# Long convolutions of a hybrid encoder block: from 64-by-64 blocks staged in DRAM to 128-by-32 points reshuffled inside SBUF

## The chip, the cores and the metric

The kernel is written in Bass for one core of a Trainium2 chip. A core has a matrix engine (TensorE, PE), VectorE (DVE), ScalarE (ACT), GpSimd (POOL), a queue engine for transfers (SP) and 16 DMA engines. The metric is the device time of one execution in microseconds, the median of several.

## The reference

One encoder block over 2048 tokens of 1024 channels. RMSNorm, a projection, then two halves of 512 channels: a two-directional gated recurrence (LRU), and an order-2 Hyena recurrence with two long convolutions. Both are normed and projected out; then a mixture of 32 experts (top 2 within one of four groups) and a last RMSNorm.

```python
k = concat([hf, zeros(1), hb[1:][::-1]])        # 4096 taps, 2 orders, 512 channels
k = k / (sum(abs(k), axis=0) + EPS);  kf = rfft(k)
def _long_conv(z, kf, skip):
    y = irfft(rfft(z, n=2 * seq) * kf, n=2 * seq)[:, :seq]
    return y + z * skip
z = x1 * _long_conv(v, kf[:, 0], skip[0])
z = x2 * _long_conv(z, kf[:, 1], skip[1])
```

`hf` and `hb` come from a small network with sines over 33 features per position, times a decay. `v`, `x1` and `x2` are three-tap depthwise convolutions of the projection.

## The kernel before

The program is a row of phases. Each has a program for every engine, held together by counting semaphores, and begins by clearing its semaphores, so no phase overlaps the next. SP issues DMAs in the order written, and a wait on SP holds back all that stands behind it.

- `load_and_norm` (L83): norms x, turns it into `hT` and runs the sine network, whose result `zz` goes to DRAM (`ZZ`, L131). The 33 rows of `feats` are its first load (L118).
- `project_and_lru` (L226): four channel tiles, in each five projections of 8 x 4 products of 128x128 by 128x512 (`fill`, L361), gates, two scans, and the three-tap convolutions (`hyena_conv`, L491). The results v, x1, x2 are transposed and go to DRAM as `L`: three arrays of [128, 16, 512]; tile l holds tokens 16 p + l in row p.
- `filters` (L529): reloads `zz`; for each of 32 tiles GpSimd spreads it over a masked `zb` (L582), TensorE makes the taps of both orders (`generate`, L609), VectorE multiplies with the decay (L660) and takes the magnitude (L663), GpSimd sums it (L589), TensorE transforms (`transform`, L615), ScalarE copies (L639) and stores `KA`. At the end VectorE forms the reciprocal norm `invn`.
- For each of the two orders three phases. `conv_forward` (L671): 32 products over the points n1, results to DRAM as `SA`. `conv_blocks` (L717): 32 blocks, in each a load of five tables (`mats`, L743), z and k (`zin`, `kin`, L745) of 128 rows of 2 KB, then five full products (L758, L763, L764), two multiplications by the spectrum on VectorE (L803), a copy and a store of `qo` to DRAM (`SI`). `conv_inverse` (L806): `stage` is loaded back, two products per tile (L840), scale by `invn`, add the skip, apply the gate, and in order 1 transposes and a store of `YT`.
- `output_projection` (L977): 16 tiles. SP loads `yt` and the rows of x (`xt`, L1036, L1051), TensorE makes 48 split products per tile, VectorE adds x (L1186) after it has waited once for five small loads of router weights, biases and gain (`w_in_`, L1029, L1214).
- `route`, `experts`: not touched.
- `combine` (L1600): 16 tiles, for each a load of x2 (`xcomb`, L1621), two indirect gathers of expert rows (L1645), sums, norm, and a store of 512 KB to the output (L1627) with two buffers.

## Time and profile before

| | us |
|---|---|
| median of 3 runs | 2717.03 (2716.83 to 2722.48) |
| profiled execution | 2722.55, span 2720.8 |

| engine | busy us | share of the span |
|---|---|---|
| PE | 2319.1 | 85% |
| DVE | 1418.7 | 52% |
| ACT | 1067.5 | 39% |
| POOL | 316.8 | 12% |

The profile counts 531.74 MB of transfers, 195 GB/s over the span. An f32 product of 128x512 is recorded as two matrix instructions. "DMA share" is the mean busy share of the 16 DMA engines; packets are booked by their start, so a short stretch can show over 1. Time stamps are microseconds from the span's start.

### The profile page before, as it was taken

To read this page: it belongs to the slowest core of one execution; us is meant where nothing else is said; L and a number is where in the kernel's file an instruction comes from. 1 tells how busy PE (TensorE), PEld (TensorE's weight loads), DVE (VectorE), ACT (ScalarE), POOL (GpSimd) and SP (SyncE) were. 2 spreads that over 40 slices of the span, in tenths; PEclk is the share of its full clock that TensorE was granted. 3 is DMA by queue.
4 is the path that set the end of the run, shared out by engine and by line. 5 is a ranking of instruction groups with operands and counts; after the bars stand their busy time and mean duration, and the time that the engine had idled before them with its cause. 6 is when DMAs were issued, how large, how long until landed. Compare 5 with 4: busy or idle time off the path is not lost. (4 is left out here: it accounts for less than half of the span.)

```text
span 2720.8 us, 33071 instructions
## 1 busy us (share of the span) xinstructions
PE 2319.1 (85%) x8253; PEld 1455.2 (53%) x8254; DVE 1418.7 (52%) x1238; ACT 1067.5 (39%) x1342; POOL 316.8 (12%) x337
## 2 busy tenths in 40 slices
PE   2699999999879599679849994699999999999940
PEld 1344444444333244234327873588878788788830
DVE  4357291745679123312244445446486864655447
ACT  4232221414122322032222221456586965766533
POOL 0000000000078300420120000000000000000023
PEclk8899999999989799789869997799999999999975
DMA  3122313121266488378743431667598986786648
GB/s 152 34 79 64 100 47 108 33 73 58 62 214 217 173 276 280 143 276 290 276 173 111 153 136 57 246 230 290 220 388 310 395 310 240 277 309 217 261 185 355
DMA packets 263770, 531.74 MB, mean 195 GB/s; under 512 B 27311, under 2 KB 98195, under 8 KB 259347
## 3 DMA queue, kind: packets, MB, share of 16 engines
q1 hardware_dynamic: 221812, 390.76, 41.1%
q10 hardware_dynamic: 30112, 97.53, 9.0%
q0 software_dynamic: 11808, 43.00, 4.2%
q8 instruction: 17, 0.28, 0.0%
q14 instruction: 21, 0.17, 0.0%
HBM read 390.69 MB, written 140.51 MB: 195 GB/s over the span
## 5 line engine op out<-in xcount | busy, mean ns | idle before, releaser
L361 PE MATMUL pj<-hT,W 128*128 128x512 f32 x1280 | 553.7, 594 | 2.7 <-DMA W<-in_w_in_dram 2.7
L361 PEld LDWEIGHTS pj<-hT,W 128*128 128x128 f32 x1280 | 243.0, 191 | 304.3 <-issue 304.3
L1458 PE MATMUL p<-wh_hi,x_hi 128*128 128x512 f32 x768 | 309.0, 402 | 11.2 <-DVE wh_lo L1583 11.1
L1583 DVE TENSOR_TENSOR wh_lo<-w_raw,wh_hi 128x2048 fp32r<-128x2048 f32 x128 | 284.8, 2287 | 51.5 <-ACT wh_hi L1547 48.8
L1458 PE MATMUL p<-wh_lo,x_hi 128*128 128x512 f32 x768 | 304.2, 396 | 0.0
L1458 PE MATMUL p<-wh_hi,x_lo 128*128 128x512 f32 x768 | 304.1, 396 | 0.0
L1547 ACT ACTIVATE wh_hi<-w_raw 128x2048 fp32r<-128x2048 f32 x128 | 234.7, 1914 | 0.3 <-DMA w_raw<-in_exp_w_dram 0.2
L803 DVE TENSOR_TENSOR u<-pr,zs 128x512 f32<-128x512 f32 x64 | 44.3, 692 | 287.4 <-ACT zs L778 167.5
L1458 PEld LDWEIGHTS p<-wh_hi,x_hi 128*128 128x128 f32 x768 | 144.6, 188 | 49.5 <-DVE wh_lo L1583 15.0
L1458 PEld LDWEIGHTS p<-wh_hi,x_lo 128*128 128x128 f32 x768 | 144.7, 188 | 35.0
L1458 PEld LDWEIGHTS p<-wh_lo,x_hi 128*128 128x128 f32 x768 | 144.8, 189 | 32.7
L1458 PE MATMUL pyy<-wy_hi,a_hi 128*128 x392 | 160.0, 408 | 2.3 <-ACT yb L1529 2.3
L1458 PE MATMUL pyy<-wy_lo,a_hi 128*128 x392 | 155.5, 397 | 0.0
L1458 PE MATMUL pyy<-wy_hi,a_lo 128*128 x392 | 155.3, 396 | 0.0
L1583 DVE TENSOR_TENSOR wy_lo<-w_raw,wy_hi 128x2048 fp32r<-128x2048 f32 x64 | 143.6, 2285 | 0.0
L1594 DVE TENSOR_TENSOR a<-p,s 128x512 f32<-128x512 f32 x48 | 33.2, 692 | 204.2 <-ACT s L1556 204.2
L406 ACT ACTIVATE hraw<-pj 128x512 f32<-128x512 f32 x48 | 28.7, 597 | 265.1 <-PE pj L361 265.1
L1547 ACT ACTIVATE wy_hi<-w_raw 128x2048 fp32r<-128x2048 f32 x64 | 119.3, 1911 | 2.4 <-DMA w_raw<-in_exp_w_dram 1.5
L1428 POOL COPY curidx<-idx 128x1 int32 (+1 forms) x50 | 9.1, 183 | 870.3 <-PE px L1466 795.3
L1556 ACT ACTIVATE s<-p 128x512 f32<-128x512 f32 x48 | 28.9, 601 | 207.6 <-PE p L1458 207.3
L758 PE MATMUL pz<-zin,mats 128*128 128x512 f32 x128 | 67.9, 613 | 32.8 <-DMA kin<-scratch_KA 32.8
L783 ACT ACTIVATE qo<-pq 128x512 f32<-128x512 f32 x64 | 38.2, 597 | 139.0 <-PE pq L764 139.0
(266 smaller groups left out, 3796.2 us busy)
## 6 DMA issues: line engine op xcount, KB each, us to landing
w_raw<-in_exp_w_dram SPq DMA_DIRECT2D x512, 256.0 KB, 4.6
w_raw<-in_exp_w_dram SPq DMA_DIRECT2D x128, 512.0 KB, 9.6
scratch_YB<-yb ACTq DMA_DIRECT2D x50, 512.0 KB
mats<-in_mats_dram SPq DMA_DIRECT2D x64, 320.0 KB, 3.2
scratch_YB<-zero SPq DMA_DIRECT2D x4, 4096.0 KB, 14.6
scratch_KA<-kst ACTq DMA_DIRECT2D x32, 512.0 KB, 3.5
scratch_SA<-stage ACTq DMA_DIRECT2D x8, 2048.0 KB, 6.7
zin<-scratch_SA SPq DMA_DIRECT2D x64, 256.0 KB, 4.1
```

The source lines that it names most:

```text
L361: last = pe.matmul(pj[n][:, :], lhs(k), rhs(k, n), start=(k == 0), stop=(k == n_k - 1))
L406: ins = act.activation(out(n), pj[n][:, :], func)
L758: pe.matmul(bank_[s % 2][:, :], mats[:, s, m, :], rhs[:, s, :], start=True, stop=True).then_inc(fwd, 1)
L783: act.activation(qo[:, s, :], pq[s % 2][:, :], ACT.Copy).then_inc(q_evac, 1)
L803: dve.tensor_tensor(dst[:, s % 2, :], src[s % 2][:, :], zs[:, s % 2, :], ALU.mult).then_inc(uv_ready, 1)
L1428: pool.tensor_copy(cur[:, :], idx[:, ds(B + LEAD, 1)]).then_inc(idx_ready, 1)
L1458: mm = pe.matmul(acc[:, :], x[:, k, :], w, start=(k == 0 and i == 0), stop=(k == n - 1 and i == 2))
L1547: act.activation(place, raw[:, j:j + 2, :], ACT.Copy).then_inc(rounded, 1)
L1556: act.activation(s1[:, :], p1[:, :], ACT.Silu).then_inc(s_ready, 1)
L1583: dve.tensor_tensor(lo, raw[:, j:j + 2, :], hi.bitcast(F32), ALU.subtract).then_inc(lowered, 1)
L1594: dve.tensor_tensor(a[:, :], p3[:, :], s1[:, :], ALU.mult).then_inc(a_ready, 1)
```

## The change

1. Order of phases: `load_and_norm`, `filters`, `project_and_lru`, one phase `conv`, `output_projection` and on. `zz` stays in SBUF, laid out twice with zeros (`zzd`), so nothing is masked or reloaded. The magnitude moves to ScalarE, in one instruction for both orders. The skip is added to tap 0 in units of the norm, and 1/norm is folded into the taps of x1 and x2 in `project_and_lru`.
2. 4096 points are 128 by 32 instead of 64 by 64. Tiles are l of 16, tokens 32 n + 2 l + g in row (g, n); the three-tap convolutions write in that order (`by_parity`), and x and the output are read and stored through the same order, as `[2, 64, 1024]`.
3. `conv`: both orders in one phase. Forward products have 64 rows of contraction, spectrum products 64 output columns, so that each uses half of the array, in pairs. 16 pairs per order; the tables (2 MB forward, 2 MB inverse) are loaded once.
4. `stage` ([128, 32, 512]) stays in SBUF. A pair's signal is copied from four partitions of it to 128 partitions of `zin`, twice per pair, the result back to four partitions, twice per pair. `KA` is read as four rows of 64 KB in the same way.

```diff
-            act.activation(zz[0:R, :], arg[0:R, :], ACT.Sin).then_inc(mlp_sin, 1)
+            act.activation(zzd[0:R, 0, :], arg[0:R, :], ACT.Sin).then_inc(mlp_sin, 1)
...
-                    conv(step, hc[:, slot, :], hraw[:, slot, :], 3, Q_HW + which, 3, Q_HB + which, hc_ready)
+                    conv(step, hc[:, slot, :].rearrange("p (g m) -> p g m", g=2), hraw[:, slot, :],
+                         3, Q_HW + which, 3, Q_HB + which, hc_ready, by_parity)
...
+                dve.tensor_tensor(tile(j), pk[j % 2][:, :, :], dec[:, j % 4, :].unsqueeze(1).broadcast_to([P, 2, CH]), ALU.mult).then_inc(k_ready, 1)
...
+        def rows(a, p, t):
+            first = (p & 1) * 64 + (p >> 1 & 1) * 32 + t * 16 + (p >> 2)
+            return a[first:first + 13:4]
...
+            def load_k(n):
+                for t in range(2):
+                    sp.dma_start(kin[:, n % 3, t, :], rows(dram["KA"][n // PAIRS], n % PAIRS, t)).then_inc(kin_in[n % 3], 16)
+
+            def load_z(n):
+                for t in range(2):
+                    sp.dma_start(zin[:, n % 3, t, :], rows(stage, n % PAIRS, t)).then_inc(zin_in[n % 3], 16)
+
+            def store_q(n):
+                sp.wait_ge(q_evac, n + 1)
+                for t in range(2):
+                    sp.dma_start(rows(stage, n % PAIRS, t), qo[:, n % 2, t, :]).then_inc(q_out[n % 2], 16)
+
+            def blocks(o):
+                sp.wait_ge(a_act, NT * (o + 1))
+                sp.wait_ge(a_dve, NT * (o + 1))
+                for n in range(o * PAIRS, o * PAIRS + 3):
+                    load_z(n)
+                for n in range(o * PAIRS, o * PAIRS + PAIRS):
+                    sp.wait_ge(z_mm, 2 * n + 2)
+                    if n + 3 < (o + 1) * PAIRS:
+                        load_z(n + 3)
+                    if n + 3 < 2 * PAIRS:
+                        sp.wait_ge(k_mm, n + 1)
+                        load_k(n + 3)
+                    if n > o * PAIRS:
+                        store_q(n - 1)
+                store_q((o + 1) * PAIRS - 1)
...
+            def spread(bank, t, src, free):
...
+                for g in range(2):
+                    h = slice(g * HALF, g * HALF + HALF)
+                    pe.matmul(bank[:, g, :], fs[h, :], src[h], start=True, stop=True).then_inc(a_mm, 1)
...
+            def k_product(n):
...
+                for r in range(2):
+                    for t in range(2):
+                        h = slice(t * HALF, t * HALF + HALF)
+                        last = pe.matmul(pk[n % 2][h, r, :], fwd[:, 2 * p + t, r * HALF:r * HALF + HALF], kin[:, n % 3, t, :], start=True, stop=True)
...
+            def inverse(n):
...
+                for r, y, done in ((0, yr, yr_ready), (1, yi, yi_ready)):
+                    pe.wait_ge(done, n + 1)
+                    for t in range(2):
+                        h = slice(t * HALF, t * HALF + HALF)
+                        last = pe.matmul(pq[:, t, :], inv[h, p, r, :], y[h, n % 2, :], start=(r == 0), stop=(r == 1))
...
+                for r, out in ((0, by_r), (1, by_i)):
...
+                    dve.tensor_tensor(out[:, n % 2], pk[n % 2][:, :, :], zs[:, n % 2, r, :].unsqueeze(1).broadcast_to([P, 2, CH]), ALU.mult).then_inc(prod, 1)
...
-        x_t = dram["x"].rearrange("o (p l) d -> l p (o d)", l=NT)
+        x_t = dram["x"].rearrange("o (n l g) d -> l g n (o d)", g=2, l=NT)
...
-        out_t = dram["out"].rearrange("o (p l) d -> l p (o d)", l=NT)
+        out_t = dram["out"].rearrange("o (n l g) d -> l g n (o d)", g=2, l=NT)
...
-                sp.dma_start(out_t[ds(t, 1)].rearrange("a p d -> (a p) d"), out[:, q % 2, :]).then_inc(o_out[q % 2], 16)
+                sp.dma_start(out_t[ds(t, 1)].rearrange("a g n d -> (a g) n d"), out[:, q % 2, :]).then_inc(o_out[q % 2], 16)
```

In order, the one phase loads tables, four groups of `L` and the first three k (`ring` holds three groups of four tiles), spreads v into `stage` (16 tiles), runs the 16 pairs of order 0, then alternates `collect` (inverse over n1, times the gate) with the next `spread`, runs the 16 pairs of order 1, and collects again with transposes and the store of `YT`. GpSimd makes the real part of the product from the two products of VectorE, which makes the imaginary part.

## Rows read from the trace of the kernel before

**Rows 1.** Busy time by stage: stretch, length, then each engine's us (instructions), clock, DMA.
```profile
core 0: us, PE busy (x) PEld busy (x) DVE busy (x) ACT busy (x) POOL busy (x), PEclk, DMA share, GB/s
...
90.00:760.00 670.00, 631.69 (x1623) 292.42 (x1621) 357.12 (x156) 168.69 (x232) 3.50 (x8) 0.97 0.24 71
...
749.70:905.00 155.30, 123.69 (x260) 48.35 (x260) 132.13 (x134) 38.23 (x64) 109.34 (x98) 0.92 0.57 200
...
905.00:947.00 42.00, 30.23 (x64) 13.00 (x64) 0.00 (x0) 18.46 (x32) 20.31 (x16) 0.83 0.51 208
947.00:1099.00 152.00, 140.64 (x320) 61.79 (x320) 42.12 (x64) 38.22 (x64) 0.00 (x0) 0.95 0.79 262
1099.00:1142.00 43.00, 30.50 (x64) 13.16 (x64) 21.88 (x32) 0.00 (x0) 24.26 (x16) 0.82 0.49 198
...
1422.00:1672.00 250.00, 230.05 (x1182) 191.52 (x1182) 104.78 (x184) 65.87 (x127) 17.87 (x30) 0.98 0.36 123
...
2625.00:2720.80 95.80, 0.00 (x0) 0.00 (x0) 63.79 (x80) 31.89 (x56) 39.32 (x32) 0.50 0.91 356
```

**Rows 2.** Waits in the block part, 947 to 1099: who waited, us, times, longest.
```profile
ACT qo L783 <- PE pq L764: 69.5, 32, 2.8
...
PE pz L758 <- DMA kin<-scratch_KA: 16.5, 1, 16.5
```

**Rows 3.** Timeline: starts of phases, of VectorE's splits, and combine's first store.
```profile
749.70 0.34 SPq L560 DMA_DIRECT2D zz<-scratch_ZZ  x1
...
903.69 0.34 SPq L683 DMA_DIRECT2D faz<-in_fa_signal_dram  x1
...
1397.54 2.12 SPq L1032 DMA_DIRECT2D wo<-in_w_out_dram  x4
...
1414.17 0.74 DVE L1210 TENSOR_SCALAR wo_hi<-wo,gAB 128x1024 fp32r<-128x1024 f32 x1
...
2625.21 0.34 SPq L1619 DMA_DIRECT2D gain_fin<-in_norm_final_g_dram  x1
...
2645.31 0.36 SPq L1627 DMA_DIRECT2D out_dram<-outt  x1
```

**Rows 4.** Groups of instructions: projection and filters; busy us, mean ns, idle before.
```profile
L361 PE MATMUL pj<-hT,W 128*128 128x512 f32 x1280 | 553.7, 594 | 2.7 <-DMA W<-in_w_in_dram 2.7
...
L663 DVE SCALAR_TENSOR_TENSOR ka<-kt 128x512 f32<-128x512 f32 x64 | 85.1, 1329 | 4.3
L589 POOL TENSOR_TENSOR acc<-acc,ka 128x512 f32<-128x512 f32 x64 | 81.1, 1267 | 24.3 <-DVE ka L663 24.3
...
L660 DVE TENSOR_TENSOR kt<-pk,dec 128x512 f32<-128x512 f32 x64 | 43.4, 679 | 11.2 <-PE pk L609 11.2
...
L639 ACT ACTIVATE kst<-pa 128x512 f32<-128x512 f32 x64 | 38.2, 597 | 114.2 <-PE pa L615 114.2
```

**Rows 5.** Groups of instructions: the same VectorE shape, strided and contiguous.
```profile
L524 DVE TENSOR_TENSOR Tb<-Tf,If 128x2048 f32<-128x2048 f32 x4 | 15.1, 3773 | 58.0 <-ACT If L406 58.0
...
L520 DVE TENSOR_TENSOR Tf<-Tf,Tb 128x2048 f32<-128x2048 f32 x4 | 9.2, 2293 | 0.1
```

**Rows 6.** DMA issues: transfer, issuer, count, KB each, median us to landing.
```profile
mats<-in_mats_dram SPq DMA_DIRECT2D x64, 320.0 KB, 3.2
...
zin<-scratch_SA SPq DMA_DIRECT2D x64, 256.0 KB, 4.1
kin<-scratch_KA SPq DMA_DIRECT2D x64, 256.0 KB, 4.6
scratch_SI<-qo ACTq DMA_DIRECT2D x64, 256.0 KB, 4.2
...
xt<-in_x_dram SPq DMA_DIRECT2D x16, 512.0 KB, 5.1
...
out_dram<-outt SPq DMA_DIRECT2D x16, 512.0 KB, 5.5
```

**Rows 7.** Stretches: `feats` in flight, loads of X, experts, combine; columns as in rows 1.
```profile
5.00:5.60 0.60, 0.00 (x0) 0.00 (x0) 0.00 (x0) 0.00 (x0) 0.00 (x0) 1.00 0.77 288
14.00:18.00 4.00, 4.00 (x6) 1.65 (x5) 0.00 (x0) 0.00 (x0) 0.00 (x0) 1.00 1.02 418
...
1972.00:2040.00 68.00, 67.36 (x312) 54.30 (x310) 57.35 (x38) 57.74 (x51) 4.60 (x8) 1.00 1.03 388
...
2640.00:2700.00 60.00, 0.00 (x0) 0.00 (x0) 46.79 (x60) 23.71 (x42) 31.76 (x24) 0.50 1.02 395
```

More of the change, by code:

```diff
@@ L22 @@
 R = 64
-HALF = R // 2
+N1, N2 = P, N // P
+HALF = N1 // 2
+PAIRS = N2 // 2
 NT = 16
@@ new lines, in _, with magnitude, evacuate @@
+        @block.scalar
+        def _(act):
+            def magnitude(j):
+                act.wait_ge(k_ready, j + 1)
+                if j >= 2:
+                    act.wait_ge(summed, j)
+                act.activation(ka[:, j % 2], tile(j), ACT.Abs).then_inc(abs_ready, 1)
+            def evacuate(i):
+                act.wait_ge(fa_done, i + 1)
+                if i >= 4:
+                    act.wait_ge(kst_out[i % 4], 16 * (i // 4))
+                act.activation(kst[:, i % 4], pa[i % 2][:, :, :], ACT.Copy).then_inc(kst_ready, 1)
+            magnitude(0)
+            magnitude(1)
+            for j in range(2, N2):
+                magnitude(j)
+                evacuate(j - 2)
+            evacuate(N2 - 2)
+            evacuate(N2 - 1)
@@ new lines, in z_product @@
+            def z_product(n):
+                p = n % PAIRS
+                pe.wait_ge(zin_in[n % 3], 32 * (n // 3) + 32)
+                if n:
+                    pe.wait_ge(zs_ready, 2 * n)
+                for r in range(2):
+                    for t in range(2):
+                        h = slice(t * HALF, t * HALF + HALF)
+                        last = pe.matmul(pz[h, r, :], fwd[:, 2 * p + t, r * HALF:r * HALF + HALF], zin[:, n % 3, t, :], start=True, stop=True)
+                    last.then_inc(z_mm, 1)
@@ new lines, in blocks, with collect @@
+            def blocks(o):
+                first = o * PAIRS
+                k_product(first)
+                for n in range(first, first + PAIRS):
+                    z_product(n)
+                    if n + 1 < first + PAIRS:
+                        k_product(n + 1)
+                    if n > first:
+                        inverse(n - 1)
+                inverse(first + PAIRS - 1)
+            def collect(out, l, free):
+                if free > 0:
+                    pe.wait_ge(gated, free)
+                for g in range(2):
+                    h = slice(g * HALF, g * HALF + HALF)
+                    last = pe.matmul(out[h, :], ia[:, :], stage[:, 2 * l + g, :], start=True, stop=True)
+                last.then_inc(i_mm, 1)
@@ new lines, in _ @@
+            pe.wait_ge(tables_in, 32)
+            for l in range(NT):
+                if l % 4 == 0:
+                    pe.wait_ge(ring_in[l // 4 % 3], 16 * (l // 12) + 16)
+                spread((*pk, pz, pq)[l % 4], l, ring[:, l // 4 % 3, l % 4, :], l - 3)
+            pe.wait_ge(fwd_in, 16)
+            pe.wait_ge(a_act, NT)
+            pe.wait_ge(a_dve, NT)
+            pe.wait_ge(inv_in, 16)
+            blocks(0)
+            for s in range(2):
+                pe.wait_ge(q_out[s], 32 * (PAIRS // 2))
@@ new lines, in _ @@
+            LAG = 2
+            for l in range(NT + LAG):
+                if l < NT:
+                    collect(pq[:, l % 2, :], l, l - 1)
+                if l >= LAG:
+                    t = l - LAG
+                    pe.wait_ge(gated, t + 1)
+                    spread((pz, *pk)[t % 3], t, z[:, t % 4, :], NT + t - 2 if t >= 3 else 0)
+            pe.wait_ge(a_act, 2 * NT - 2)
+            pe.wait_ge(a_dve, 2 * NT - 2)
+            blocks(1)
+            for s in range(2):
+                pe.wait_ge(q_out[s], 32 * PAIRS)
@@ new lines, in result, with blocks @@
+            def result(n):
+                act.wait_ge(inv_mm, n + 1)
+                if n >= 2:
+                    act.wait_ge(q_out[n % 2], 32 * (n // 2))
+                act.activation(qo[:, n % 2], pq[:, :, :], ACT.Copy).then_inc(q_evac, 1)
+            def blocks(o):
+                first = o * PAIRS
+                for n in range(first, first + PAIRS):
+                    signal(n)
+                    if n > first:
+                        result(n - 1)
+                result(first + PAIRS - 1)
@@ new lines, in gate @@
+            def gate(out, t, G0, free):
+                G = G0 + t // 4
+                dve.wait_ge(i_mm, (G0 // GROUPS - 1) * NT + t + 1)
+                dve.wait_ge(ring_in[G % 3], 16 * (G // 3) + 16)
+                if t >= 4:
+                    dve.wait_ge(free, 2 * (NT + t - 3) if free is a_mm else t - 3)
+                dve.tensor_tensor(z[:, t % 4, :], out, ring[:, G % 3, t % 4, :], ALU.mult).then_inc(gated, 1)
+            for l in range(NT):
+                evacuate((*pk, pz, pq)[l % 4], l, l)
```

677 lines of the change are left out of this document (298 added, 379 removed).

## The prediction

> **What bounds the kernel now.** I read the busy time by stage first [rows 1]. The change touches five of these stages. The filters (749.7 to 905) keep VectorE busy 132 of 155 us and TensorE 124. A long convolution has a forward part (42 us), a block part (152 us) and an inverse part (43 us); the second repeats it. In the block part TensorE is busy 141 of 152 us at a DMA share of 0.79, so it is TensorE's stage with DMA close behind. The waits say the same: ScalarE waits for the product, and the only long wait for a transfer is the first, 16.5 us [rows 2]. The forward and inverse parts have TensorE busy 30 us of 42 to 43; the rest is the start of a phase. The output projection (1422 to 1672) is TensorE's, with DMA at 0.36. The last stage, combine, has DMA at 0.91 over its whole length and no TensorE work: there the transfers set the time. Projection with the LRU (90 to 760) is TensorE's, 632 of 670 us.
>
> **Filters, moved ahead of the projection.** The zero-padded `zz` makes the masked copies on GpSimd unnecessary. A tile still needs two generating and two transforming products. A full f32 product of 128x512 is two records; 1280 of them take 553.7 us, so one product costs 0.865 us [rows 4] and a tile 3.46 us. Before, VectorE set the pace with two of 0.68 and two of 1.33 us = 4.0 us [rows 4]. The magnitude now goes to ScalarE and VectorE keeps about 1.36 us a tile; GpSimd has 2 x 1.27 = 2.5, ScalarE about 2 x 0.6 + 1.1 = 2.3 (the kst row, and its like for the magnitude). TensorE becomes the bound: 32 x 3.46 = 111 us. Around it: some 8 us for loads and first tiles, and a tail that is new, because tile 0 is transformed only after the norm: last product, magnitude, sum, ones products, eight small ones, the skip added, transform, store: about 18 us; then 4 us to the next phase. 141 us, against 154 from 749.7 to 903.7 [rows 3]: **-13 us** (-25 to +10). The store of ZZ and its reload go; they lay in the head of the old stage.
>
> **Projection.** The same products. VectorE reads its three-tap convolutions at a stride of two. Its one strided operation here takes 3.79 us against 2.29 for a contiguous one of the same shape [rows 5], so a convolution may cost up to 4 us more, three times per channel tile. VectorE is busy 357 of 670 us [rows 1], and the last operation of each tile waits 58.0/4 = 14.5 us for a gate that TensorE makes last [rows 5]. That idle time hides 12 us: 0 (0 to +10 if the cover fails in one tile). The folding of the norm into the taps is two tiny operations in the setup: 0.
>
> **Long convolutions: what TensorE saves.** Before, 32 blocks of five products, 4.3 us each, twice: 280 us of TensorE [rows 1]. Now 16 pairs with four spectrum, four signal and four inverse products that each use half of the array. If the two halves run together a pair costs 6 x 0.865 = 5.2 us, if not 10.4 us. Nothing in this trace shows two half-array products side by side. The mats (64 x 320 KB [rows 6]) go too. The Trainium skill, TensorEngine Tiling (Array Packing), Key Properties, says that tiles run loads and products in parallel, and that changing the tiling mode drains the engine; no run here shows either.
>
> **Long convolutions: what the transfers cost.** Here is the point on which I decide. Each pair moves z in, k in and q out as 2 x 256 KB each, and each of these DMAs has one side of only **four rows** (four partitions of `stage`, or four rows of `KA`) of 64 KB, where the old ones had 128 rows [rows 6]. The trace has one large transfer with few rows, the 33 rows of `feats`: in its fullest stretch it moved 288 GB/s, where four 2 MB loads of 128 rows move 418 [rows 7]. 288/418 is 11.0 of 16, and 11 is the largest divisor of 33 up to 16. So I read: the outermost dimension is dealt out evenly, and a DMA of four rows gets four engines, always with the others idle. The other reading (33 rows are just a short burst) would leave all 16. The Trainium skill, DMA: Bandwidth & Descriptors, Why a DMA increments its semaphore by 16 and not by 1, states it: the engine count is the largest up to 16 that divides the slowest dimension of both sides, and the lowest-numbered engines are used. The 288 GB/s agree; by its rule the change loses what the shared engines lose, and this speaks against the change.
>
> The price: 192 DMAs of 256 KB are 50.3 MB. Saturated 2 KB and 4 KB traffic moves 388 GB/s [rows 7], 24.2 per engine, so four engines move 97 GB/s and need 520 us. The same engines also carry their sixteenth of 12 MB of L, 4 MB of tables and 4 MB of YT, 21 MB at 395 to 418 GB/s: 51 us. Where these engines stand still: 7 us at the start, 5 at the end of the first spread (its last ring slot is queued behind six k loads), 10 and 12 at the two block tails where z, products, inverse and store follow one another, 28 in the middle collect and spread (16 tiles of about 2 us less its ring loads), 25 in the last collect with transposes and 3 for landings: 90 us. Together 661 us. Before, from 903.7 to 1397.5 [rows 3], 494 us. **+167 us**. Ends: 20.7 GB/s per engine (block part: 262/16/0.79 [rows 1]) gives 608 in place of 520, +255; 26.1 (418/16) gives 482, +129. TensorE's 5.2 or 10.4 us per pair lie under 16 us of transfer, and so do VectorE (2 x 1.36 + 0.68), ScalarE (2.3) and GpSimd (1.3). If the halves do not run together only the spreads and collects grow, by about 60 us.
>
> What waits behind: SP issues everything in order. A z load waits for `z_mm`, a k load for `k_mm`, and the store of q behind both; three z and three k are ahead, 32 us of queue, so a stall of TensorE is not felt.
>
> **Output projection.** x is now read as [2, 64, 1024], two outer rows: by the same reading two engines, 256 KB each, at 24.2 to 26.1 GB/s 10 to 10.6 us; with a sixteenth of 1.5 MB of other traffic on the same engines 14 us a tile, against 250/16 = 15.6 us. A load is issued after the tile two before it is done and has about 18 us until VectorE adds it, so in the steady state it just hides. At the start two such loads stand ahead of the router weights and the gain on SP's queue, for all of which VectorE waits: wo 10 + x 20 + yt 5 us from 1400 makes 1436 to 1438, where the eight splits of wo, 2 us each from 1414, end near 1430 [rows 3]: **+8 us** (0 to +50).
>
> **Combine.** The output is stored as [2, 64, 1024] too. Before, 32 MB at 395 GB/s [rows 7] was the bound. On the two engines a tile now is 256 KB of store, 32 KB of x and 64 KB of gathered rows: 352 KB at 25 GB/s, 14 us. From the first store, 20 us into the stage [rows 3], 16 stores of 10.4 us, 12 loads of 1.3 and some 22 gathers of 1.3: 166 + 16 + 26 = 208 us. 228 us against 95.8: **+132 us** (+110 to +150; 0 if the store uses all engines).
>
> **Sum.** -13 + 0 + 167 + 8 + 132 = +294 us. The profiled execution took 2722.6 us (span 2720.8), the median is 2717.0; on the median this gives **3011 us**. Nothing in experts or routing changes: the tiles hold other tokens, but the slots of the experts are as many.
>
> **Rivals.**
> All sixteen engines take every DMA (the 33 rows mislead). A pair is then 1.57 MB at 262 GB/s [rows 1], 6.0 us, above TensorE's 5.2: 192 us, with 95 us for spreads, collects and transposes and 35 us of starts and tails 322: -172, filters -13, nothing else: 2532 us. For it: the full stretch of those 33 rows lasts 0.6 us, one sample. Against it: 288 GB/s where 33 rows would keep sixteen engines busy as well.
> The same, but half-array products don't overlap, so that the change doesn't do what it says: 10.4 us per pair, 333 us, and 150 + 35 around it: 518, +24 - 13: 2728 us.
> Four engines in the convolutions but all of them for x and the output (the two-row side is merged or split on the way): 2717 - 13 + 167 = 2871 us.
> The slow side beyond my sum: SBUF to SBUF copies that read one partition per engine and write another run at half the rate of the rows, 12 GB/s. 128 of the 192 DMAs (z and q) then take twice 347 us: 3011 + 347 = 3358 us. It decides as soon as one engine's rate from a single partition falls below 20 GB/s. No row shows SBUF to SBUF.
>
> **How the numbers follow.** Forecast as summed 0.66; forecast with halves that don't overlap (about 3071) 0.08; few engines only in the convolutions 0.07; half rate 0.05; sixteen engines 0.11; sixteen without overlap 0.03. The terms' ends, not all at once on one side, give 2940 to 3150 for the first two. To leave out no more than 0.2 the range takes in 2871: 2860 to 3160; outside lie the sixteen engines (0.14 in all) and the half rate (0.05). About 0.2% is what a measurement of this kernel can tell from no change: faster 0.11, within 0.01 (of the last case), slower 0.88.
>
> **What the profile would show.** The block stretches at a DMA share near 0.25 and about 97 GB/s with TensorE busy a third, and TensorE waiting for `zin`; z landing after 15 us or more instead of 4; combine near 228 us at about 150 GB/s with ScalarE waiting for the store of outt; filters near 141 us with TensorE busy all of it. The forecast is wrong if the blocks show a DMA share over 0.7, or if an x load lands in 5 us as before [rows 6].

## The result and the profile after

The changed kernel takes 2987.2 us (median), the kernel before 2719.7 us beside it: ratio 1.098, 95% interval 1.096 to 1.100. It is slower by 267 us. The profiled execution took 2989.0 us, its span is 2987.3. One of the four runs, 3459.8 us long with a granted clock of 0.70 on the mean against 0.88 in the others, is left out of the ratio; the other three lie between 2983.7 and 2989.0.

Timeline of the changed kernel, SP's queue, the first transfer of each phase (start us, us, engine and line, transfer). They answer to [rows 3]: the phases now start with the filters at 97.8 and the projection at 233.5.

```profile
97.81 1.12 SPq L564 DMA_DIRECT2D w<-in_hy_filt_w_dram  x2
...
233.50 0.34 SPq L281 DMA_DIRECT2D prow<-in_lru_conv_w_dram  x1
...
882.88 0.36 SPq L745 DMA_DIRECT2D fs<-in_fa_signal_dram  x1
...
1519.34 2.07 SPq L1095 DMA_DIRECT2D wo<-in_w_out_dram  x4
...
1801.32 0.34 SPq L1323 DMA_DIRECT2D tri<-in_tri_dram  x1
...
2761.81 0.34 SPq L1682 DMA_DIRECT2D gain_fin<-in_norm_final_g_dram  x1
```

From one start to the next, beside the kernel before and the prediction:

| stage | before | after | change | predicted |
|---|---|---|---|---|
| load and norm | 100.9 | 97.8 | -3.1 | 0 |
| filters | 154.0 | 135.7 | -18.3 | -13 |
| projection, LRU | 648.8 | 649.4 | +0.6 | 0 |
| long convolutions | 493.9 | 636.5 | **+142.6** | +167 |
| output projection | 269.8 | 282.0 | +12.2 | +8 |
| routing, experts | 957.9 | 960.5 | +2.6 | 0 |
| combine | 95.6 | 225.5 | **+129.9** | +132 |
| sum | | | +266.5 | +294 |

The changed kernel by stretch, columns as in [rows 1]: the filters, the blocks of the first convolution, the middle (collect and spread), the blocks of the second, the steady output projection, combine from its first store on, and the end of combine, where its last store is alone.

```profile
97.80:233.50 135.70, 117.64 (x276) 65.31 (x276) 42.35 (x37) 64.15 (x65) 77.52 (x37) 0.92 0.54 190
...
928.29:1195.76 267.47, 121.66 (x384) 33.95 (x384) 50.13 (x49) 35.17 (x48) 28.95 (x17) 0.72 0.28 106
1100.00:1180.00 80.00, 37.74 (x112) 10.77 (x112) 12.19 (x12) 10.12 (x14) 7.42 (x5) 0.71 0.26 98
1195.76:1232.02 36.26, 36.23 (x133) 9.41 (x135) 22.13 (x32) 9.55 (x16) 0.00 (x0) 0.92 0.31 103
1232.02:1477.03 245.01, 120.05 (x382) 33.44 (x379) 50.15 (x49) 35.20 (x48) 28.97 (x17) 0.73 0.26 99
...
1541.00:1791.00 250.00, 228.25 (x1146) 189.59 (x1147) 105.58 (x181) 62.42 (x122) 17.81 (x30) 0.96 0.35 126
2782.00:2938.00 156.00, 0.00 (x0) 0.00 (x0) 46.95 (x60) 22.77 (x40) 28.21 (x22) 0.50 0.45 154
...
2975.00:2987.00 12.00, 0.00 (x0) 0.00 (x0) 0.00 (x0) 0.00 (x0) 0.00 (x0) 0.50 0.12 49
```

Read the blocks against [rows 1]: there TensorE was busy 141 of 152 us with DMA at 0.79 and 262 GB/s. Now no engine is busy half of the time, and DMA, which looks idle at 0.26, is the bound: 0.26 of sixteen is four engines. Combine fell from 0.91 and 356 GB/s to 0.45 and 154. Its 0.45 is no count of engines, since the loads of x2 and the gathered rows are in it; the last store, alone, shows 0.12 and 49 GB/s, two engines of sixteen.

Waits of the changed kernel, first in the blocks of the first convolution (928 to 1195), then in the whole of combine (who waited, us, times, longest):

```profile
PEld ck L788 <- DMA kin<-scratch_KA: 114.7, 13, 10.0
```

```profile
ACT outt L1718 <- DMA out_dram<-outt: 150.5, 14, 16.8
```

In [rows 2] TensorE waited 16.5 us for a transfer, once. Now it waits 13 times for k, which stands behind z in SP's queue of z, k, q. That queue, one pair of blocks (timeline of SP):

```profile
1098.75 5.27 SPq L722 DMA_DIRECT2D zin<-stage  x2
1104.06 5.15 SPq L718 DMA_DIRECT2D kin<-scratch_KA  x2
1109.25 5.09 SPq L727 DMA_DIRECT2D stage<-qo  x2
```

Each group of two takes SP 5.1 to 5.3 us here, for 512 KB, and up to 5.9 elsewhere in the blocks. From 1250.33 to 1410.96 ten pairs were issued, 16.06 us a pair of 1.57 MB: 98 GB/s.

### The profile page after: what moved, and what is told of

It reads as the page before. It is cut to its first block and busy times, and to the rows that moved or that the text cites. A ratio compares the mean times of both kernels' runs of the same rounds, so it can differ in the third digit from the quotient of the medians.

```text
span 2987.3 us, 30293 instructions
## 1 busy us (share of the span) xinstructions
PE 2232.7 (75%) x8397; PEld 1389.6 (47%) x8398; DVE 1358.1 (45%) x1130; ACT 1059.8 (35%) x1262; POOL 252.3 (8%) x243
## 5 line engine op out<-in xcount | busy, mean ns | idle before, releaser
L1521 PE MATMUL p<-wh_hi,x_hi 128*128 128x512 f32 x768 | 308.9, 402 | 11.2 <-DVE wh_lo L1646 11.1
L788 PE MATMUL ck<-kin,fwd_b 128*64 128x512 f32 x256 | 106.0, 976 | 216.6 <-DMA kin<-scratch_KA 205.7
L942 DVE TENSOR_TENSOR by_r<-ck,zs 128x1024 f32<-128x1024 f32 x32 | 39.2, 1224 | 362.5 <-ACT zs L886 362.5
L892 ACT ACTIVATE qo<-cq 128x1024 f32<-128x1024 f32 x32 | 32.7, 1023 | 375.3 <-PE cq L811 326.5
L922 POOL TENSOR_TENSOR yr<-by_r,by_i 128x512 f32<-128x512 f32 x32 | 56.6, 1767 | 1170.0 <-DVE by_i L942 1170.0
L788 PEld LDWEIGHTS ck<-kin,fwd_b 128*64 128x64 f32 x256 | 23.3, 202 | 278.6 <-DMA kin<-scratch_KA 228.6
```

The source lines that it names most:

```text
L788: last = pe.matmul(pk[n % 2][h, r, :], fwd[:, 2 * p + t, r * HALF:r * HALF + HALF], kin[:, n % 3, t, :], start=True, stop=True)
L892: act.activation(qo[:, n % 2], pq[:, :, :], ACT.Copy).then_inc(q_evac, 1)
L922: dif = pool.tensor_tensor(yr[:, n % 2, :], by_r[:, n % 2, 0, :], by_i[:, n % 2, 1, :], ALU.subtract)
L942: dve.tensor_tensor(out[:, n % 2], pk[n % 2][:, :, :], zs[:, n % 2, r, :].unsqueeze(1).broadcast_to([P, 2, CH]), ALU.mult).then_inc(prod, 1)
L1521: mm = pe.matmul(acc[:, :], x[:, k, :], w, start=(k == 0 and i == 0), stop=(k == n - 1 and i == 2))
```

## The experiments

My theory was that of the prediction: the outermost dimension of a transfer's two sides sets how many DMA engines take part, as the largest number up to 16 that divides it on both sides. In every run below the smaller of the two counts divides the larger, so what happens when it does not stays open. The rivals: copies from SBUF to SBUF, or few partitions at one end, are slow in themselves; scattered rows or patterns of two levels are slow; SP's in-order issue or the half-array products hold the period. Where no ratio is given, the kernel was run once; repeated runs of one kernel lay within 0.4% of each other, 10 us, so small differences are read from the stages of the trace.

### Rows of the x loads and of the output

```diff
-                sp.dma_start(out_t[ds(t, 1)].rearrange("a g n d -> (a g) n d"), out[:, q % 2, :]).then_inc(o_out[q % 2], 16)
+                for g in range(2):
+                    sp.dma_start(out_t[ds(t, 1)][:, g].rearrange("a n d -> (a n) d"), out[64 * g:64 * g + 64, q % 2, :]).then_inc(o_out[q % 2], 16)
```

The x loads of the output projection are split alike, and the waits count two DMAs per tile.

> The changed kernel with one edit in two stages: each x load of the output projection and each output store of combine goes out as two DMAs of 64 rows instead of one of 2 x 64. The same bytes to the same addresses, twice as many DMAs. Theory (the outermost dimension of a pattern is dealt out over the engines, so two outer rows get two engines and 64 get all sixteen): combine falls from 225.5 us to the 96 us of the kernel before, the output projection from 282 to 270, nothing else moves, 2987 - 142 = 2845 us. Rival (the 4 KB rows of the output lie every 32nd row of DRAM, and that scatter or the store itself is slow): the rows lie as before, both stages stay, 2987 us. Rival (SP's issue of each DMA costs): slower by 28 x 0.6 us.

Measured: 2851.7 us against 2720.3 before, ratio 1.049 (1.047 to 1.050). Combine took 102.6 us, the output projection 273.8. Twice as many stores, and combine is less than half as long. The stretch of its combine between stores, and its longest wait:

```profile
2770.00:2830.00 60.00, 0.00 (x0) 0.00 (x0) 40.35 (x53) 21.45 (x38) 25.13 (x19) 0.50 0.99 365
```

```profile
ACT outt L1722 <- DMA out_dram<-outt: 40.5, 14, 5.3
```

The same bytes went to the same addresses, so scatter in DRAM is out. SP's issue costs nothing either. Combine kept 7 us over the kernel before: between its stores it moves 365 GB/s, where that kernel moved 395 [rows 7]. Why is open.

### Rows of k

```diff
-                    sp.dma_start(kin[:, n % 3, t, :], rows(dram["KA"][n // PAIRS], n % PAIRS, t)).then_inc(kin_in[n % 3], 16)
+                    first = (n % PAIRS) * 8 + t * 4
+                    sp.dma_start(kin[:, n % 3, t, :], dram["KA"][n // PAIRS][first:first + 4].rearrange("i n c -> (i n) c")).then_inc(kin_in[n % 3], 16)
...
+    FK = F
     F, IA = F[:, np.argsort(place)], IA[np.argsort(place)] / N
...
-    out = dict(fa_filter=F, ...)
+    out = dict(fa_filter=FK, ...)
```

> The changed kernel with KA in the natural order of the spectrum, so that four consecutive rows of 64 KB are 128 rows of 2 KB: the k loads have 128 outer rows instead of four; z and q keep four. Same bytes. Theory (four engines carry z, k and q; a pair of 1.57 MB took 15.4 us, 25.5 GB/s per engine): z and q leave 1.05 MB for the four engines, 10.3 us, and a sixteenth of k on each adds 1.3: 11.6 us a pair, 32 x 3.8 = -122 us, 2865 us. Rival (the copies from SBUF to SBUF are the slow ones, bound by the few partitions at one end, and k only waits in line behind them): the period falls by less than the 1.3 us that k would take on sixteen engines at full rate, under -45 us. Rival (SP's in-order issue, or the waits of the block chain, set the period): 0.

Measured: 2884.6 us, ratio 1.060 (1.058 to 1.062); the convolutions took 533.8 us, -102.7. The expectation was on a period of 15.4 us that I had read from too short a stretch; over ten pairs it is 16.1. Here it is 13.3. SP's queue, one pair:

```profile
1049.24 5.06 SPq L723 DMA_DIRECT2D zin<-stage  x2
1054.35 3.16 SPq L719 DMA_DIRECT2D kin<-scratch_KA  x2
1057.55 4.91 SPq L728 DMA_DIRECT2D stage<-qo  x2
```

and two stretches of such a pair, first with a k passing, then with z alone (columns as in [rows 1]):

```profile
1044.00:1048.00 4.00, 4.00 (x14) 1.09 (x12) 0.00 (x0) 0.00 (x0) 0.00 (x0) 0.74 0.60 174
1050.00:1054.00 4.00, 0.00 (x0) 0.00 (x0) 3.05 (x3) 0.48 (x1) 1.49 (x1) 0.87 0.26 98
```

k went to more engines, z and q stayed at four and at their pace. But k kept 3.2 us of the queue, not the 1.3 that its bytes need. From a block part's first z to the first ring load behind it the two parts are 46.1 and 37.6 us shorter, together 84 of the 103; the rest is the head, where six k loads stood ahead of the ring loads: the first z is issued 26.7 us after the phase starts, in the changed kernel 45.4. The rival "SBUF to SBUF" had foreseen under 45 us; it is weakened, not out.

### z issued by GpSimd

```diff
-                    sp.dma_start(zin[:, n % 3, t, :], rows(stage, n % PAIRS, t)).then_inc(zin_in[n % 3], 16)
+                    pool.dma_start(zin[:, n % 3, t, :], rows(stage, n % PAIRS, t)).then_inc(zin_in[n % 3], 16)
```

with the waits for `a_act`, `a_dve` and `z_mm` moved to GpSimd's stream.

> The changed kernel with the z loads issued by GpSimd (its software queue) instead of SP; patterns, bytes and waits are the same. Theory: all four-row DMAs of SP's queue use the same four engines. If GpSimd's queue deals its four-row DMAs to other engines, k and q keep 1.05 MB on the four, and z adds its share: 11.6 us a pair if z goes round all engines, 10.3 if it has four others, conv -120 to -160 us, 2830 to 2865 us. If GpSimd's queue uses the same four: no change in the block stretches, 15.4 us a pair. Rival (the partitions of stage are the limit, whoever issues): 15.4 us too; then the next run but one, z through DRAM, tells them apart.

Measured: 2918.6 us, the convolutions 569.0, -67.5. A stretch of its blocks:

```profile
1000.00:1100.00 100.00, 51.89 (x176) 14.65 (x172) 24.04 (x24) 16.45 (x24) 23.60 (x24) 0.76 0.39 118
```

Over 100 us the share is 0.39 and 118 GB/s pass, where with SP alone it stays at 0.26 and 98; in single stretches it is 0.54 (1058.5 to 1060), in others 0.26 (1050 to 1052). So the same four-row copies ran in part beside SP's on other engines, and the partitions of `stage` were not the limit. The Trainium skill, DMA: Bandwidth & Descriptors, Why a DMA increments its semaphore by 16 and not by 1, says that GpSimd's queue takes its engines in turn. The changing share agrees with that; which engines they were no view shows. The gain was about half of what I expected. GpSimd waited 87.5 us for TensorE's z product (12 times, 950 to 1150) before it could issue; whether that or the queue's own pace took the other half stays open.

### One prime number

The kernel before, with other shapes for its output store.

```diff
+        out_4 = dram["out"].rearrange("o (n g l) d -> l g n (o d)", l=NT, g=4)
...
-                sp.dma_start(out_t[ds(t, 1)].rearrange("a p d -> (a p) d"), out[:, q % 2, :]).then_inc(o_out[q % 2], 16)
+                if t < 12:
+                    n = (P, 127, 126)[t // 4]
+                    sp.dma_start(out_t[t][0:n], out[0:n, q % 2, :]).then_inc(o_out[q % 2], 16)
+                else:
+                    sp.dma_start(out_4[t], out[:, q % 2, :]).then_inc(o_out[q % 2], 16)
```

> The kernel before (not the changed one) with four shapes of output store in combine: tiles 0 to 3 with 128 rows as they were, 4 to 7 with 127 rows (the last row of each tile is left out), 8 to 11 with 126 rows (the last two are left out), 12 to 15 with the same 128 rows as four outer rows of 32 (rows interleaved by four, so that part of the output is in another order). The count of engines is the largest one up to 16 that divides the outermost dimension, is the theory: 127 is prime, one engine, 508 KB at 25.5 GB/s are 20 us and with that engine's share of the loads 24 us a tile; 126 gives 14 engines and is like 128, 6 us a tile; four rows give four, 5.1 us plus 3.9 of loads, 9 us, or 5.1 once no load is left. Stage 96 + 4 x 18 + about 6 = 174 us, the whole 2800 us. Rival (a pattern of two levels is slow, all engines take part): 127 and 126 are like 128, only the last four are longer, stage under 115 us, 2740 us. Rival (engines are filled in turn whatever the count): nothing changes, 2720 us.

Measured: 2813.3 us, +93; the stage 189.6 us, 16 more than expected. Timeline of its stores: the four of 127 rows, the first two of 126.

```profile
2663.22 0.28 SPq L1630 DMA_DIRECT2D out_dram<-outt  x1
2677.63 1.26 SPq L1630 DMA_DIRECT2D out_dram<-outt  x1
2699.87 0.37 SPq L1630 DMA_DIRECT2D out_dram<-outt  x1
2719.10 7.65 SPq L1630 DMA_DIRECT2D out_dram<-outt  x1
2748.66 1.39 SPq L1630 DMA_DIRECT2D out_dram<-outt  x1
2766.05 0.36 SPq L1630 DMA_DIRECT2D out_dram<-outt  x1
```

One row less, in a plain pattern of one level, and a tile takes 14 to 30 us, 21.4 on the mean ((2748.66 - 2663.22) / 4). With one more row less, once the slow ones have drained, the next two stores follow 4 us apart (2770.02, 2773.99). The rivals foresee no such step between 128 and 127 rows. The last four, of four outer rows, took 7.6 us each to the end of the span, between my two values.

### All of it through DRAM, with 128 rows and with four

Two kernels that share one edit: a spread tile of `stage` goes to a DRAM buffer SZ, z is loaded from there, q goes to SQ and comes back into `stage`. In the first SZ, KA and SQ are read and written as 128 rows, in the second with the changed kernel's four. The edit of the first:

```diff
-                    sp.dma_start(zin[:, n % 3, t, :], rows(stage, n % PAIRS, t)).then_inc(zin_in[n % 3], 16)
+                    first = (n % PAIRS) * 8 + t * 4
+                    sp.dma_start(zin[:, n % 3, t, :], dram["SZ"][first:first + 4].rearrange("i n c -> (i n) c")).then_inc(zin_in[n % 3], 16)
...
-                    sp.dma_start(rows(stage, n % PAIRS, t), qo[:, n % 2, t, :]).then_inc(q_out[n % 2], 16)
+                    first = (n % PAIRS) * 8 + t * 4
+                    sp.dma_start(dram["SQ"][first:first + 4].rearrange("i n c -> (i n) c"), qo[:, n % 2, t, :]).then_inc(q_out[n % 2], 16)
...
+                sp.dma_start(dram["SZ"][:, 2 * l:2 * l + 2, :], stage[:, 2 * l:2 * l + 2, :]).then_inc(sz_out, 16)
...
+                    sp.dma_start(stage[:, 4 * g:4 * g + 4, :], dram["SQ"][:, 4 * g:4 * g + 4, :]).then_inc(st_in[g], 16)
```

> The changed kernel without its SBUF to SBUF copies: each spread tile of stage is stored to DRAM (128 rows of 4 KB), z is loaded as 128 rows of 2 KB, q goes to DRAM as 128 rows and comes back into stage in eight loads; KA in the natural order as in e2_k128. Half-array products, one phase and everything else stay. 32 MB of transfers more. Theory (rows, hence engines): a pair is 1.57 MB on sixteen engines, 4 to 6 us, so TensorE's three groups of 1.94 us, 5.8 us, or the chain z, evacuation, products, GpSimd, inverse set the period at about 7 us instead of 15.4; spreads and collects as before, four turns of store and load cost 6 us each: conv 395 us instead of 636, 2987 - 241 = 2746 us. If the turns and the extra 32 MB weigh more, up to 2800. Rival (the half-array products or the block chain hold the period near 15 us): conv stays above 620 us, 2970 us or more.

> As e5_dram, z and q through DRAM, but every z, k and q transfer keeps the changed kernel's pattern of four outer rows of 64 KB on its DRAM side (KA in its permuted order). Nothing goes from SBUF to SBUF, and the bytes per pair are the same. Theory (four rows, four engines, wherever the rows lie): the period stays at 15.4 us a pair at 98 GB/s, and the four turns through DRAM come on top: conv 640 to 670 us, 2990 to 3020 us. Rival (a copy from SBUF to SBUF, or from and to only four partitions, is what is slow): z and q are faster here, the period falls below 12 us, the whole is under 2900 us.

Measured: with 128 rows 2717.5 us, 28 less than expected, ratio 0.9997 (0.9988 to 1.0007) to the kernel before, the convolutions 366.3 us. With four rows 3028.3 us, the convolutions 674.2. The blocks of each, 128 rows first:

```profile
965.00:1050.00 85.00, 73.91 (x304) 22.94 (x300) 39.37 (x41) 27.48 (x37) 21.24 (x12) 0.92 0.77 274
```

```profile
950.00:1180.00 230.00, 120.92 (x381) 33.71 (x382) 50.15 (x49) 34.23 (x47) 28.98 (x17) 0.73 0.26 100
```

With nothing from SBUF to SBUF the four rows give the same 0.26 and 100 GB/s, and 15.8 us a pair (z at 1061.17, 1077.01, 1092.86, 1108.63). With 128 rows a pair takes 5.5 us (z at 974.85, 980.37, 985.85), and TensorE is the bound again, busy 74 of 85 us. So the new convolutions, half-array pairs, one phase and tables loaded once together, are worth -128 us against [rows 3]'s 493.9, once the engines are there. How much of it each of the three gives was not divided.

### From SBUF to SBUF with all partitions

```diff
-                    sp.dma_start(zin[:, n % 3, t, :], rows(stage, n % PAIRS, t)).then_inc(zin_in[n % 3], 16)
+                    sp.dma_start(zin[:, n % 3, t, :], stage[:, 2 * (n % PAIRS) + t, :]).then_inc(zin_in[n % 3], 16)
```

and q back alike; k as 128 rows. The kernel leaves out the spreading of four partitions over 128, so its convolutions compute nothing meaningful.

> The changed kernel with k as in e2_k128, and with z and q still copied from SBUF to SBUF, the same bytes in as many DMAs, but partition to partition: zin takes tile 2p + t of stage with its 128 partitions in place, and q goes back there. It leaves out the transpose between partitions, so the convolution's values mean nothing; only its time counts. Theory (the four outer rows are the cause, not the memory at either end): all engines take part, the period falls from e2's 13.3 us to TensorE's 5.5 us as in e5_dram, and without the four turns through DRAM the convolutions take about 335 to 355 us, 2690 to 2705 us in all. Rival (SBUF to SBUF is slower than DRAM even with all rows): the period stays above 8 us, conv above 440 us.

Measured: 2663.1 us, the convolutions 312.8. SP's queue, one pair, 5.5 us to the next:

```profile
978.93 1.26 SPq L723 DMA_DIRECT2D zin<-stage  x2
980.24 1.09 SPq L719 DMA_DIRECT2D kin<-scratch_KA  x2
983.27 1.11 SPq L728 DMA_DIRECT2D stage<-qo  x2
```

That closes a square: SBUF or DRAM, four rows or 128. With four rows the memory moves the period by 0.3 us (16.1 and 15.8); the rows move it by 10. With 128 rows TensorE sets the 5.5 us, so a difference between the memories would not show. My lower bound of 335 was too high by 22 us; I did not divide that further.

### The law by itself

The kernel before with 18 single stores behind its last one. `to` is one tile of a scratch buffer in DRAM.

```diff
+            for n, g in ((128, 1), (127, 1), (126, 1), (121, 1), (128, 8), (125, 5), (128, 4), (126, 3), (128, 2)):
+                for _ in range(2):
+                    dst = to[0:n].rearrange("(n g) d -> g n d", g=g) if g > 1 else to[0:n]
+                    sp.dma_start(dst, out[0:n, 0, :]).then_inc(law_out, 16)
+                    done += 16
+                    sp.wait_ge(law_out, done)
```

> The kernel before, with 18 more DMAs appended after its last store: one buffer of outt goes to a scratch buffer in DRAM, one DMA at a time, each waited for before the next, two of each shape: 128 rows of 4 KB; 127; 126; 121; 128 as 8 outer rows of 16; 125 as 5 of 25; 128 as 4 of 32; 126 as 3 of 42; 128 as 2 of 64. Theory: engines = the largest number up to 16 that divides the outermost dimension of both sides, 25.5 GB/s each, and about 2 us to issue and land. From issue to the next issue: 16 engines 3.3 us; 127 rows one engine 22.4; 126 rows 14 engines 3.4; 121 rows 11 engines 3.8; eight 4.6; five 6.0; four 7.1; three 8.8; two 12.3. Together +143 us, 2863 us. Rival (two levels in a pattern are slow in themselves, the count of rows does not matter): 127, 126 and 121 rows all within 0.3 us of 128, and the five two-level shapes all alike.

Measured: 2875.2 us. A stretch inside each shape's stores, in the order 128, 127, 126, 121 rows, then 8, 5, 4, 3, 2 outer rows; the last two columns are the share of 16 engines and the GB/s (the short stretches hold a bit of a store's start or end):

```profile
2719.60:2721.00 1.40, 0.00 (x0) 0.00 (x0) 0.00 (x0) 0.00 (x0) 0.00 (x0) 0.50 0.91 375
2730.00:2740.00 10.00, 0.00 (x0) 0.00 (x0) 0.00 (x0) 0.00 (x0) 0.00 (x0) 0.50 0.06 26
2766.80:2768.00 1.20, 0.00 (x0) 0.00 (x0) 0.00 (x0) 0.00 (x0) 0.00 (x0) 0.50 0.91 311
2773.20:2775.20 2.00, 0.00 (x0) 0.00 (x0) 0.00 (x0) 0.00 (x0) 0.00 (x0) 0.50 0.68 168
2782.00:2786.00 4.00, 0.00 (x0) 0.00 (x0) 0.00 (x0) 0.00 (x0) 0.00 (x0) 0.50 0.46 113
2795.00:2799.00 4.00, 0.00 (x0) 0.00 (x0) 0.00 (x0) 0.00 (x0) 0.00 (x0) 0.50 0.31 98
2808.50:2816.50 8.00, 0.00 (x0) 0.00 (x0) 0.00 (x0) 0.00 (x0) 0.00 (x0) 0.50 0.22 61
2829.00:2836.00 7.00, 0.00 (x0) 0.00 (x0) 0.00 (x0) 0.00 (x0) 0.00 (x0) 0.50 0.19 64
2850.00:2860.00 10.00, 0.00 (x0) 0.00 (x0) 0.00 (x0) 0.00 (x0) 0.00 (x0) 0.50 0.12 47
```

The shares fit 16, 1, 14, 11, 8, 5, 4, 3 and 2 sixteenths, within the idle edges; 126 rows can't be told from 128 here. But the times from issue to issue are as expected only at the ends: 2.6 (3.3 expected), 22.3 (22.4), 3.1 (3.4), 4.3 (3.8), 6.1 (4.6), 6.9 (6.0), **10.2 (7.1)**, 9.9 (8.8), 12.9 (12.3). Four rows cost more than three. Two runs more were for this.

```diff
-                    dst = to[0:n].rearrange("(n g) d -> g n d", g=g) if g > 1 else to[0:n]
+                    dst = dram["X2"][0:g, 0:n // g] if g > 1 else dram["X2"][0][0:n]
```

> As e9_law, with one difference: the five shapes of two levels write blocks of rows to DRAM (8 blocks of 16 adjacent rows, 5 of 25, 4 of 32, 3 of 42, 2 of 64, each block in another tile of the scratch buffer), where in e9_law row i of block b lay next to row i of block b + 1, so that engines wrote neighbouring 4 KB rows at once. In e9_law the share of busy engines followed the count (0.22 to 0.25 for four) but four rows took 10.2 us instead of the 7.1 expected, and eight 6.1 instead of 4.6. Theory (the interleaved rows slow each engine, the count stands): here 8 rows take 4.6 us or less, five 5.5, four 6.5, three 8.3, two 11.8, from 1.3 us plus 25 GB/s per engine; the five pairs save about 17 us in all. Rival (a pattern of four or eight outer rows is slow per engine wherever the rows lie): the five times are those of e9_law: 6.1, 6.9, 10.2, 9.9, 12.9 us.

Measured: 2876.1 us, and from issue to issue 6.1, 7.0, 10.2, 9.9 and 12.9 us: the same. My guess that neighbouring rows in DRAM disturb each other was wrong, its rival right.

```diff
-                for _ in range(2):
+                for r in range(4):
...
-                    sp.wait_ge(law_out, done)
+                sp.wait_ge(law_out, done)
```

(each of the four to a place of its own)

> As e11_law_blocks, but four DMAs of each shape go out one behind the other, to different places, and only the fourth is waited for: 36 DMAs. e11_law_blocks gave the same times as e9_law, so the place of the rows in DRAM is not what made four rows take 10.2 us where 25.5 GB/s per engine give 5.1 + 1.3, while in the convolutions four-row DMAs queued behind each other moved 98 GB/s. Theory (the loss is at the start of a DMA that finds its engines idle): a group of four takes 1.3 us, four times the full-rate time, and the loss once: eight rows 14 us, five 19, four 26, three 30, two 44; one engine (127 rows) 85, sixteen 6.5; all nine groups 240 us, 2960 us. Rival (each engine is slower in these shapes, whatever is queued): four times the single time: eight 20.5, five 24, four 37, three 36, two 48; 283 us, 3003 us.

Measured: 2958.2 us. A group of four took 6.4, 81.5, 8.4, 10.4 us (128, 127, 126, 121 rows), then 14.7, 19.9, 25.5, 29.8 and about 43 us (8, 5, 4, 3, 2 outer rows): as the theory said. Stretches inside the groups of 128 and of 126 rows, then of the group of four outer rows, first its beginning and then its steady part:

```profile
2718.00:2722.00 4.00, 0.00 (x0) 0.00 (x0) 0.00 (x0) 0.00 (x0) 0.00 (x0) 0.50 1.03 421
2806.00:2811.00 5.00, 0.00 (x0) 0.00 (x0) 0.00 (x0) 0.00 (x0) 0.00 (x0) 0.50 0.88 305
2860.00:2864.00 4.00, 0.00 (x0) 0.00 (x0) 0.00 (x0) 0.00 (x0) 0.00 (x0) 0.50 0.25 51
2866.00:2880.00 14.00, 0.00 (x0) 0.00 (x0) 0.00 (x0) 0.00 (x0) 0.00 (x0) 0.50 0.26 105
```

Queued, 126 rows are told from 128: 0.88 is 14 of 16. And the loss, 3.8 us with four outer rows, is seen: in the first 4 us the four engines are busy all the time but move 51 GB/s, later 105. The single store of four rows before did the same, 50 GB/s at a share of 0.25 from 2808.5 to 2812.5, and its last 2 us passed at 0.12, with two of the four engines already done. So the loss falls once, at the start of a group that finds its engines idle. Behind others a four-row transfer costs its bytes over four engines, as in the convolutions. Why each engine is slow at first stays open.

### The pace of the filters

```diff
-                act.activation(ka[:, j % 2], tile(j), ACT.Abs).then_inc(abs_ready, 1)
...
+                for o in range(2):
+                    last = dve.scalar_tensor_tensor(out=ka[:, j % 2, o], in0=tile(j)[:, o, :], scalar=-1.0, in1=tile(j)[:, o, :], op0=ALU.mult, op1=ALU.max)
+                last.then_inc(abs_ready, 1)
```

> The changed kernel with one edit in the filters: the magnitude of each tile is taken by VectorE again (two scalar_tensor_tensor of 128x512, 1.33 us each before) instead of ScalarE. Theory (before, VectorE set the pace of the filters with 4.0 us a tile, and the change frees it, so that TensorE's 3.46 us set it): VectorE has 1.36 + 2.66 = 4.0 us a tile again, the stage goes from 135.7 to about 8 + 32 x 4.05 + 17 = 155 us, +19 us, the whole 3006 us. Rival (the gain of 18 us is the store and reload of zz and the head of the stage, not the pace): stage within 4 us of 136.

Measured: 2996.0 us. The stage took 147.0 us (95.65 to 242.69), in the changed kernel 135.7: +11.3, neither the +19 nor the rival's 0 to 4. Its VectorE groups in the filters:

```profile
L659 DVE SCALAR_TENSOR_TENSOR ka<-kt 128x512 f32<-128x512 f32 x64 | 76.1, 1228 | 1.1
...
L654 DVE TENSOR_TENSOR kt<-fk,dec 128x1024 f32<-128x1024 f32 x32 | 38.7, 1211 | 13.0 <-PE fk L592 13.0
```

2 x 1.23 + 1.21 = 3.67 us a tile, against 4.0 before [rows 4]: the magnitude costs 0.2 us a tile less, and the merged decay product over 1024 columns 0.15 less than two over 512. So this kernel does not bring back the pace of before: its 32 tiles take VectorE 113.6 us (104.09 to 217.72), there 128.3 (761.36 to 889.70). Of its own 11.3 us over the changed kernel, 8 are there when the sums over the taps begin (220.29 and 214.35, 124.6 and 116.5 us into the stage). The other 3 follow there: TensorE has waited 3 us, and its products for the norm take 7.0 us at a granted clock of 0.50, where the changed kernel took 3.7 at 1.00:

```profile
220.29:227.29 7.00, 6.96 (x20) 4.81 (x20) 0.00 (x1) 0.00 (x0) 0.00 (x0) 0.50 0.04 17
```

So taking the magnitude off VectorE is worth 11 of the 18 us. The other 7 are a balance that this kernel shows against the one before: the first product with the decay comes 8.4 us after the stage's start, not 11.7; the tiles take 14.7 us less; and what follows them takes 25.0 us, not 14.0. What of it goes back to zz, no longer stored and loaded, was not tried by itself, nor were the 3 us in load and norm.

### Both ends together

The DRAM version with 128 rows and the split x loads and output stores:

> e5_dram with the two edits of e1_rows64: every large transfer has at least 64 outer rows. If the theory holds the gains add, since they lie in different stages: e1_rows64 took 136 us off the changed kernel, e5_dram is expected to take 241 off: 2610 us, 109 us below the kernel before. If it comes out above 2719 the half-array convolutions lose even with all engines at work.

Measured: 2585.3 us against 2717.6, ratio **0.951** (0.950 to 0.953), the convolutions 367.1 us, the output projection 270.2, combine 103.2. Its blocks:

```profile
970.00:1040.00 70.00, 61.24 (x260) 19.49 (x256) 33.53 (x33) 25.11 (x34) 19.49 (x11) 0.95 0.73 247
```

The rest of the change is worth 132 us. The row counts of z, k, q, x and the output had cost 2987 - 2585 = 402 us, more if one counts what the way through DRAM adds.

## Why the prediction was right, point by point

The sum was +294 us, the spans differ by 266.5. Of the 28 us between them 24 are the convolutions; the other stages are off by at most 5 us each, in both directions.

- **What bounds each stage.** Right. The deciding point, that four outer rows get four engines, held in every run that touched it. The single row of before that it stood on, 288 GB/s for 33 rows [rows 7], was a fair sample: 121 rows, which have 11 as a divisor too, kept 0.68 of the engines. That row's own DMA share is 0.77, nearer to 12 engines than to 11; I read the count from the GB/s alone, and with one sample of 0.6 us that was partly luck. The Trainium skill, DMA: Bandwidth & Descriptors, Why a DMA increments its semaphore by 16 and not by 1, states this rule, with 127 partitions on one engine as an example; the run with 127 rows agrees at 26 GB/s.
- **Convolutions**, +167 predicted, +142.6. The rate was right: 98 GB/s against 97. The term mis-sized is the 90 us in which I let the four engines stand still, or the 51 for shared traffic, or both. The two block parts took 267.5 + 245.0 = 512.5 us, where my terms make 504 of transfers (the first six k loads lie in the head) and 22 of tails. Head, middle and last part took 45.4 + 36.3 + 42.3 = 124.0 us, where they make 135 with those six. Tails and spreads overlap with the queue more than I allowed.
- **TensorE's saving.** Four half products take 1.94 us (31.0 us over 16 groups at L799; two full ones would be 1.73, [rows 4]), so the halves do run together. In the versions with all engines a pair of twelve half products takes 5.5 us, 5.2 forecast, where one after another they would need 10.4. The groups in the blocks of the changed kernel:

```profile
L788 PE MATMUL ck<-kin,fwd_b 128*64 128x512 f32 x128 | 53.8, 990 | 114.2 <-DMA kin<-scratch_KA 103.3 <-DMA inv_b<-in_inv_b_dram 10.9
L799 PE MATMUL cz<-zin,fwd_b 128*64 128x512 f32 x128 | 31.0, 605 | 3.4 <-DMA zin<-stage 3.4
```

  The same shape costs 990 ns at L788, behind the waits of up to 10 us, and 605 at L799. The granted clock of these blocks is 0.72 on the mean, between the levels of 1.2 and 2.4 GHz, where it was 0.95 before [rows 1]. It costs nothing here, since the transfers bound the period.
- **Which wait.** I had written that TensorE would wait for `zin`. It waits for `kin`, which is queued behind z. The mechanism is the same, the name was wrong. TensorE was busy 122 of 267 us, not a third, because its records are longer at the lower clock.
- **Combine**, +132 predicted, +129.9. Right in size and mechanism: stores every 13.7 us, 14 predicted, at 154 GB/s, and the last one on two engines. A slip is in the sum: 22 gathers of 1.3 us are 29 us, not 26, which makes +135.
- **Output projection**, +8 predicted, +12.2. The place was right: the first two x loads stand ahead of the router's weights and the gain. The queue at that point, and VectorE's wait for what it loads:

```profile
1558.65 0.43 SPq L1092 DMA_DIRECT2D gain_ffn<-in_norm_ffn_g_dram  x1
```

```profile
DVE st L1225 <- DMA gain_ffn<-in_norm_ffn_g_dram: 11.1, 1, 11.1
```

  The gain is issued 39 us after the stage begins; my sum had it landed there at 38.5 to 40.5, and VectorE waits 11.1 us for it. With x loaded in 64 rows the stage is 8.2 us shorter, and from the DRAM version to the one with both ends together 11.6. In the steady part two-row x loads hide, as forecast: TensorE is busy 228 of 250 us, against 230 [rows 1].
- **Filters**, -13 predicted, -18.3. The bound moved to TensorE as said (117.6 of 135.7 us). The 32 tiles took 111.8 us, from 102.58 to 214.35, against 111; head and tail took 24, not 30.
- **Rivals.** Sixteen engines, few engines only in the convolutions, half rate from SBUF to SBUF and halves that don't overlap are each contradicted by a run above.

## What to carry to other kernels

Before a transfer is reshaped, write down the outermost dimension of both of its sides, and take the largest number up to 16 that divides both as the number of DMA engines that will carry it: four rows of 64 KB are four engines however large the rows are, and 127 rows are one. A DMA share that stays near a fixed number of sixteenths, with every compute engine waiting for transfers, is the sign of it in a profile; a low share is not a free resource, and other transfers in the stage can hide the count, as in combine. Here the smallest cure was to split one DMA of 2 x 64 rows into two of 64, which took 136 us off, and a reshuffle that has to go through DRAM to get 128 rows was still 270 us cheaper than one that stays in SBUF with four.

## What the runs showed that I had not expected

- A few-row store that finds the engines idle loses time once: 3.8 us with four outer rows (10.2 us where 1.3 us and 25.5 GB/s per engine make 6.4), 2.2 with eight, 1.9 with three, 1.6 with five, 1.3 with two and with 121 plain rows; with 128 rows none. With four outer rows the engines are busy from the start but move half as much in the first 4 us. Queued behind others a store does not lose it. It does not depend on where the rows lie in DRAM.
- A 128-row transfer between four-row ones costs more than its bytes: k took 3.2 us of the queue between z and q, where its bytes over all engines need 1.3. That the change of shape costs it is a guess; no run divides it.
- From SBUF to SBUF, partition to partition with all 128 rows, the copies were fast enough for TensorE's 5.5 us a pair, as those through DRAM were, and the convolutions were 54 us shorter without the turns through DRAM (312.8 and 366.3 us).
